# The eight remainders of the inverse transform's channel tiles move from VectorE to GpSimd

## The reference, cut to what matters

```
s = (v * x1).astype(jnp.float32)
g = hyena_filter(L, ...)                      # divided by its sum of magnitudes
y = jnp.fft.irfft(jnp.fft.rfft(s, n=n, axis=1) * jnp.fft.rfft(g, n=n, axis=0)[None], n=n, axis=1)[:, :L]
y = (y + s * skip.astype(jnp.float32)).astype(u.dtype) * x0
return y @ w_out + b_out
```

## Time and profile before

| | |
|---|---|
| median of 3 runs | 2532.64 us (2532.15, 2532.64, 2538.05) |
| profiled execution, its own time | 2537.66 us |
| its span in the profile | 2535.2 us |
| mean granted TensorE clock | 0.985 of full |
| TensorE busy | 2429.3 us (96%) |
| VectorE busy | 1124.9 us (44%) |
| GpSimd busy | 705.3 us (28%) |
| ScalarE busy | 634.2 us (25%) |

### The profile page before, as it was taken

The page is one execution under the profiler, slowest core; times in us unless marked ns, Lnnn a source line. Parts: engine busy times, 40 slices in busy tenths (PEclk is TensorE's granted clock), DMA queues, the critical chain, the costliest instruction groups (busy, mean ns, idle before and its releaser), DMA issues.

```text
span 2535.2 us, 28807 instructions
## 1 busy us (share of the span) xinstructions
PE 2429.3 (96%) x11294; PEld 1959.1 (77%) x11294; DVE 1124.9 (44%) x1181; ACT 634.2 (25%) x768; POOL 705.3 (28%) x394
## 2 busy tenths in 40 slices
PE   7999999979999999999998899999999999999996
PEld 5767766547888888888887698989897887778885
DVE  6755543254266116622347763627272123420533
ACT  4433423342211000100113544444453001111111
POOL 2221233322233333333334122121212332333331
PEclk9999999999999999999999899999999999999998
DMA  4122354681222122211112202011113322111331
GB/s 148 34 100 100 117 190 158 196 236 42 75 92 90 50 75 99 83 50 66 47 47 73 92 26 74 26 67 33 67 33 119 138 79 67 54 42 66 99 117 66
DMA packets 69969, 217.62 MB, mean 86 GB/s; under 512 B 6662, under 2 KB 16584, under 8 KB 69642
## 3 DMA queue, kind: packets, MB, share of 16 engines
q1 hardware_dynamic: 57002, 178.88, 21.4%
q10 hardware_dynamic: 12896, 37.75, 4.0%
HBM read 171.52 MB, written 45.09 MB: 85 GB/s over the span
## 4 chain that ended last, share of the span: by engine, by line
PE 72%; DVE 4%; ACT 1%; issue 0%; ACTq 0%; DVEq 0%
PE ps L1208 61%; PE ps L541 5%; DVE T L1888 1%; PE ps L1479 1%; PE ps L588 1%; PE ps L609 1%; PE ps L608 1%; PE ps L570 1%; PE ps L607 1%; PE ps L1230 0%; DVE X L2227 0%; DVE XN L1918 0%; PE ps L1239 0%; PE ps L512 0%; ACT T L1771 0%; DVE H L1911 0%
## 5 line engine op out<-in xcount | busy, mean ns | idle before, releaser
L1208 PE MATMUL ps<-H,whi 128*128 128x512 f32 x4000 | 1086.6, 394 | 21.9 <-DVE H L1955 13.1
L1208 PEld LDWEIGHTS ps<-H,whi 128*128 128x128 f32 x4000 | 751.2, 189 | 195.1 <-issue 25.1
L1162 POOL CAST whi<-wraw 128x1024 fp32r<-128x1024 f32 x190 | 201.3, 1059 | 1703.6 <-PE ps L1208 805.9
L1208 PE MATMUL ps<-H,wlo 128*128 128x512 f32 x2000 | 617.9, 390 | 0.0
L1164 POOL TENSOR_TENSOR wlo<-wraw,whi 128x1024 fp32r<-128x1024 f32 x194 | 492.1, 2536 | 58.4 <-ACT whi L675 43.1
L1208 PEld LDWEIGHTS ps<-H,wlo 128*128 128x128 f32 x2000 | 376.6, 188 | 78.9
L1208 PE MATMUL ps<-A,whi 128*128 128x512 f32 x1472 | 397.7, 393 | 8.9 <-DVE A L2259 4.9
L1208 PEld LDWEIGHTS ps<-A,whi 128*128 128x128 f32 x1472 | 278.1, 189 | 68.4 <-issue 5.3
L1208 PE MATMUL ps<-A,wlo 128*128 128x512 f32 x736 | 228.3, 392 | 0.0
L1208 PEld LDWEIGHTS ps<-A,wlo 128*128 128x128 f32 x736 | 139.2, 189 | 29.1
L2143 DVE TENSOR_TENSOR T<-ps,T 128x1024 f32<-128x1024 f32 x22 | 26.9, 1224 | 155.8 <-PE ps L1208 155.8
(11 more groups left out here) (337 smaller groups left out, 2500.8 us busy)
## 6 DMA issues: line engine op xcount, KB each, us to landing
wraw<-in_panels SPq DMA_DIRECT2D x181, 512.0 KB, 3.5
mw<-in_modp SPq DMA_DIRECT2D x24, 512.0 KB, 3.5
g<-gsp SPq DMA_DIRECT2D x16, 512.0 KB, 3.2
wraw<-g SPq DMA_DIRECT2D x16, 512.0 KB, 5.9
bs<-s SPq DMA_DIRECT2D x16, 512.0 KB, 4.9
y<-yi ACTq DMA_DIRECT2D x32, 256.0 KB, 5.2
kf<-in_kfft SPq DMA_DIRECT2D x16, 320.0 KB, 3.1
X<-in_xT SPq DMA_DIRECT2D x4, 1024.0 KB, 11.0
```

The lines of the kernel that those rows point to most:

```text
L1162: nc.gpsimd.tensor_copy(whi[:, s, :, :], wraw[:, s, :, :]).then_inc(hi_made, 1)
L1208: last = mm(p[:, c * step:(c + 1) * step], w[:, ws, k, :], operand(act, a, k, c * step, step), start=(q == 0 and w is whi and a == 0), sto ...
```

## The change

The eight subtractions leave VectorE's program. They are written into GpSimd's program, behind the splits of the first two panels of `wout` and ahead of the split of the third. For this the loop over pairs of panels is cut in two. Operands, semaphores and waits of the subtraction are the same, and so is everything else.

```diff
+assert N0["wout"] % 2 == 0
...
-            rest(1, V_PANEL // 2)
+            rest(1, N0["wout"] // 2 + 1)
+            for e in range(KT):
+                pool.wait_ge(y_hi, e + 1)
+                nc.gpsimd.tensor_tensor(A[:, 1, e, :], TT[2 + e % 2][:, :], A[:, 0, e, :].bitcast(F32), ALU.subtract
+                                        ).then_inc(y_lo, 1)
+            rest(N0["wout"] // 2 + 1, V_PANEL // 2)
...
-            def y_lo_of(e):
-                dve.wait_ge(y_hi, e + 1)
-                V_.tensor_tensor(A[:, 1, e, :], TT[2 + e % 2][:, :], A[:, 0, e, :].bitcast(F32), ALU.subtract
-                                 ).then_inc(y_lo, 1)
-
             for e in range(KT):
...
                 V_.tensor_tensor(y[:, :], y[:, :], G0[:, e, :], ALU.mult).then_inc(y_made, 1)
-                if e:
-                    y_lo_of(e - 1)
-            y_lo_of(KT - 1)
```

## The result

The changed kernel takes 2541.89 us (median of 6 runs, 2538.57 to 2546.46) against 2535.52 us for the kernel before (6 runs, 2532.15 to 2538.05). The ratio is 1.0026, 95% interval 1.0015 to 1.0037: slower, by 4 to 9 us. The profiled execution took 2540.32 us with a span of 2538.5.

The account below looks back on a forecast made before the run. VectorE's chain was taken to hold up TensorE in the first panel. With turns at 4.64 us a tile, TensorE's work moves from 582.51 to 592.0, 9.5 us later: 2532.64 + 9.5 = 2542.1 us, range 2534.5 to 2546.0.

Parts of the forecast that it names:

- What bounds the place: At the projection's first panel TensorE waits for VectorE's scaled sum, product and remainder, 3.78 us a tile before the change.
- GpSimd's queue: Remainders stand behind the weight splits of two panels; remainder 0 ends at 558.25, and 3.8 us are lost at the start.
- The allowance for entering new code: GpSimd's cost of leaving one loop and entering straight code: up to 1 us allowed, nothing taken.
- The two engines take turns: VectorE's product and GpSimd's remainder share an SBUF port pair; the earlier start holds it for the whole instruction.
- the third case: Remainder and product run side by side, two y buffers set 3.08 us a tile: 2531.2 to 2533.2 us; chance 0.12.
- Who comes first: GpSimd's remainder starts 0.07 us ahead of VectorE's next product at each tile, making the pace 4.64 us a tile.
- The case with VectorE first: VectorE's product slips in first at some tiles, two tiles taking 8.25 us instead of 9.28: 2539.0 us; chance 0.20.
- The clock: TensorE's clock is at half speed behind the last wait of the first panel, losing 2.0 us as before.
- The worse case: GpSimd starts up to 1 us later or TensorE's clock stays low longer: 2543 to 2546 us; chance 0.08.
- The sum: TensorE's work after the first panel's last k's begins at 592.0 instead of 582.51, a loss of 9.5 us.
- Reaching the end whole: Behind the first panel TensorE has no gap for 92 us, so the 9.5 us delay reaches the kernel's end.

Follow-up runs that it names:

- psum_sum: The changed kernel with the scaled sum written back into its PSUM tile and the gate's product reading it there; 2532.61 us, ratio 0.9986.
- late_hi: The changed kernel with GpSimd released by a one-element ScalarE operation behind the cast instead of the cast itself; 2540.87 us, ratio 1.0013.
- wait_twice: The changed kernel with one more, long-met wait (for y_made) before each remainder on GpSimd; 2539.48 us, ratio 1.0013.
- two_once: The changed kernel with remainders 0 and 1 back on VectorE and GpSimd's wait for them only before remainder 2; 2541.30 us, ratio 1.0023.

## Why the prediction was right

- **What bounds the place.** Right: TensorE's last k of the first panel is released by GpSimd instead of VectorE.
- **GpSimd's queue.** Right in kind. The remainders took 2.34 to 2.40 us undisturbed. I had remainder 0 end 12.45 us after the first scaled sum (558.25 - 545.80). It ended at 11.1, as scaled sum 2 at 555.90 shows, though it had to stand behind product 1: the weights' splits lay 1.3 us earlier relative to the first scaled sum in this execution (first cast 0.14 us ahead of it, before 1.17 behind it). I had taken the same distance as before, and I had not seen that remainder 0 would meet product 1. That is most of why the last remainder ended at 41.1 and not 42.8 us. The allowance for entering new code was not needed: the first remainder starts as the last split ends, in `psum_sum` too, where no product holds it up (553.18, with two remainders done in 4.68 us).
- **The two engines take turns.** Right, and shown by `psum_sum`. The rule of the Trainium skill, page "SBUF — State Buffer", section "Who interferes with whom" (the pair of ports is held for a whole instruction, the earlier start decides), is borne out by the products of 1.22, 2.0 and 3.4 us. Sharing in proportion, the third case, is excluded by `late_hi` and `wait_twice`: a shift of some 0.1 us in GpSimd's start moves a product by 2.2 us (3.4 to 1.22). The third case itself, side by side, is what `psum_sum` makes: its last remainder was priced at 579.7 - 545.80 = 33.9 us and came at 33.2.
- **Who comes first.** Right: a lead of 0.05 to 0.06 us for 0.07, a pace of 4.60 to 4.64 for 4.64. It was the step with the thinnest margin. The case with VectorE first exists (one more wait makes it), and its price was near: two tiles in 8.1 to 8.3 us for 8.25, 3.1 us priced and 3.4 won in `wait_twice`.
- **The clock.** Right in kind, low in size: 2.0 us taken, 1.37 + 1.19 + 0.30 = 2.9 measured against 1.36 us for a k. The worse case took 0.68 us for each further k at 1.2 GHz; by its own rows it is 2.73 - 1.38 = 1.35.
- **The sum.** 9.5 predicted, 8.6 in the place, 6.4 between the medians, and 6.6 and 8.4 by the two ratios. Two misses cancel in part: the last wait ended 1.7 us sooner than predicted (41.1 for 42.8), and the clock took 0.9 us more. The median came out at 2541.89 for 2542.1. That nearness is luck: the baseline of six runs was 2.9 us above that of three, and on it the same sum gives 2535.52 + 9.5 = 2545.0, 3.1 too much.
- **Reaching the end whole.** The runs agree with it, as far as intervals of about 5 us can: in all ten kernels the change of the second panel's addition lies within the interval of the ratio, in `two_once` at its edge (2.8 us in the place, 2.8 to 9.1 by the ratio).

## What to carry to other kernels

Before an operation goes from VectorE to GpSimd, count the SBUF operands of what VectorE does meanwhile: with two, the engines took turns here, and the work adds up instead of running side by side. Taking one of them from PSUM cost 0.01 us and ended it; two more buffers at least let the turns follow each other. Where two engines race for the same thing in a loop, look at who starts first in the trace, to 0.05 us, before reading a cause into a change of pace.

## What I had not expected of the hardware

- A second wait, long met, costs a GpSimd instruction 0.07 us at its start (0.14 after the cast for 0.07), and in `wait_twice` that ended the last remainder 2.1 us sooner.
- A stopped instruction ends 1.07 to 1.09 us after the other's end on VectorE, where the undisturbed one takes 1.22. I read it so that some 0.15 us of its start is done while it stands still; no run tests this.
- The scaled sum written back to PSUM takes 1.29 us, to SBUF 1.28.
- The granted clock near 1430 falls in the profiles of some kernels and not in those of others, with the same code there: 27.3, 28.9 or 30.6 us for the same work.
